# RWKV recurrence with 64x128 products of the write vectors, two VectorE steps that align the diagonal blocks, and another order of two GpSimd steps

## What is computed

```python
def step(state, inp):
    r_t, w_t, k_t, v_t, a_t, b_t = inp
    sa = jnp.einsum('bhvk,bhk->bhv', state, a_t)
    state = (state * w_t[:, :, None, :] + sa[..., None] * b_t[:, :, None, :]
             + v_t[..., None] * k_t[:, :, None, :])
    return state, jnp.einsum('bhvk,bhk->bhv', state, r_t)
```

## Time and profile before

| | |
|---|---|
| median of 3 runs | 1754.0 us (1753.24 to 1755.06) |
| the profiled execution | 1754.57 us, of which the traced span is 1752.8 us |
| PE busy | 1654.6 us, 94% of the span |
| DVE, ACT, POOL busy | 764.3, 561.3 and 452.3 us |
| mean granted clock of PE | 0.986 of full speed |
| first and last M0 of the recurrence | 153.0 and 432.5 us from the span's start |

### The profile page before, as it was taken

The page is one execution under the profiler, slowest core; times in us unless marked ns, Lnnn a source line. Parts: engine busy times, 40 slices in busy tenths (PEclk is TensorE's granted clock), DMA queues, the critical chain, the costliest instruction groups (busy, mean ns, idle before and its releaser), DMA issues. The chain is left out here.

```text
span 1752.8 us, 35509 instructions
## 1 busy us (share of the span) xinstructions
PE 1654.6 (94%) x15497; PEld 863.8 (49%) x15690; DVE 764.3 (44%) x1045; ACT 561.3 (32%) x883; POOL 452.3 (26%) x236
## 2 busy tenths in 40 slices
PE   4998889899999998899999999999999999999997
PEld 2455666666644555444444345444444444444443
DVE  5696555556425555312210388331323323222328
ACT  5323444444324555321212256321212112121200
POOL 2221322222110112022422123551423233232310
PEclk9999999999999999999999999999999999999999
DMA  9851001000101200411210211330202020212002
GB/s 358 285 175 32 15 6 38 4 27 27 28 25 49 61 1 1 137 44 36 72 36 24 96 49 37 103 129 21 85 20 76 24 72 26 70 36 84 1 0 97
DMA packets 105777, 109.75 MB, mean 63 GB/s; under 512 B 2592, under 2 KB 82610, under 8 KB 105394
## 3 DMA queue, kind: packets, MB, share of 16 engines
q1 hardware_dynamic: 105648, 107.82, 19.0%
HBM read 101.52 MB, written 4.19 MB: 60 GB/s over the span
## 5 line engine op out<-in xcount | busy, mean ns | idle before, releaser
L218 PE MATMUL tokens_ps<-a_hi,z 128*128 128x512 bf16 x878 | 228.5, 379 | 0.9
L674 PE MATMUL ff_ps<-ff_hi,c_lo 128*128 128x512 bf16 x503 | 190.6, 379 | 0.6
L674 PE MATMUL ff_ps<-ff_hi,c_hi 128*128 128x512 bf16 x501 | 189.9, 379 | 1.3 <-DVE z L2582 0.9
L674 PE MATMUL ff_ps<-ff_lo,c_hi 128*128 128x512 bf16 x501 | 189.9, 379 | 0.6
L2582 DVE TENSOR_TENSOR z<-ff_ps,z 128x512 f32<-128x512 f32 x128 | 88.3, 690 | 205.1 <-PE ff_ps L674 204.4
L2478 ACT ACTIVATE ff_r<-tokens_ps,cols 128x1024 f32<-128x1024 f32 x30 | 33.4, 1113 | 421.4 <-PE tokens_ps L218 414.4
L2404 POOL TENSOR_TENSOR z<-z 128x1024 bf16<-128x1024 f32 x28 | 62.1, 2219 | 345.5 <-ACT z L2400 345.5
L218 PEld LDWEIGHTS tokens_ps<-a_hi,z 128*128 128x128 bf16 x896 | 87.7, 98 | 105.7
L2570 DVE TENSOR_TENSOR ff_r<-ff_r 128x1024 f32<-128x1024 f32 x32 | 41.1, 1284 | 219.4 <-ACT ff_r L2478 219.4
L218 PE MATMUL tokens_ps<-a_lo,z 128*128 128x512 bf16 x438 | 131.1, 379 | 0.5
L195 POOL TENSOR_TENSOR mg_wlo<-mg_stage,mg_whi 128x1024 bf16<-128x1024 f32 x21 | 45.7, 2178 | 158.2 <-ACT mg_whi L191 158.2
(11 more groups left out here) (395 smaller groups left out, 3114.2 us busy)
## 6 DMA issues: line engine op xcount, KB each, us to landing
ff_st<-w_ff SPq DMA_DIRECT2D x8, 2048.0 KB, 7.7
z<-w_ff SPq DMA_DIRECT2D x30, 512.0 KB, 4.0
ada_w<-w_ada SPq DMA_DIRECT2D x6, 2048.0 KB, 8.3
z<-w_in SPq DMA_DIRECT2D x18, 512.0 KB, 4.9
z<-w_ada SPq DMA_DIRECT2D x8, 1024.0 KB, 13.4
mg_stage<-w_in SPq DMA_DIRECT2D x16, 512.0 KB, 3.9
zs_stage<-w_in SPq DMA_DIRECT2D x8, 512.0 KB, 7.3
ada_w<-w_ada SPq DMA_DIRECT2D x4, 1024.0 KB, 13.5
```

The lines of the kernel that those rows point to most:

```text
L218: last = pe.matmul(out[:, h * HALF:(h + 1) * HALF], w[:, kt, :], a[:, slot, h * HALF:(h + 1) * HALF], start=(x == 0 and y == 0), stop=(x = ...
L674: last = pe.matmul(out, a[:, slot, at], w[:, x, n], start=(x == 0 and y == 0), stop=(x == k - 1 and y == 2))
```

## The change

The 16 matmuls of L1808 and the 32 of L1817 become 16 matmuls of 64x128: each write vector of a chunk meets both read vectors, a and r, over all 64 tokens. The result therefore lies in the layout that M2 has, and VectorE reads it with another stride. The lower half of the rows has its diagonal block in columns 32 to 63 only. VectorE copies it over with two new operations ahead of L1507: `X` becomes the right half times a 0/1 column that keeps the lower rows, and the left half of `NTd` becomes itself times the opposite column, plus `X`. On GpSimd `dense_low(t + 2)` stands ahead of `low(t - 3)`.

```diff
--- before.py
+++ after.py
@@ -982,9 +982,9 @@
         zt, ysb, yc = sb("zt"), [sb(f"ysb{f}") for f in range(2)], [sb(f"yc{f}") for f in range(2)]
         BA, BB, BC, BD, F, TL, HY0, HY1 = (bank(n) for n in "main0 main1 inv invx front tail state0 state1".split())
         BAB, BCD, HY = (BA, BB), (BC, BD), (HY0, HY1)
-        per_turn = {"M1e": 2, "NTd": 2, "NTm": 2, "PQa": NT, "M2e": 2, "TTm": 2, "T12e": 2, "ze": 2, "ge": 2, "ysb": 2, "PQ": 2, "TTe": 4, "Te": 5, "X": 4, "Xe": 4, "TX": 4,
+        per_turn = {"nd": 2, "M1e": 2, "NTd": 2, "NTm": 2, "PQa": NT, "M2e": 2, "TTm": 2, "T12e": 2, "ze": 2, "ge": 2, "ysb": 2, "PQ": 2, "TTe": 4, "Te": 5, "X": 4, "Xe": 4, "TX": 4,
                     "ch": NC, "S": NC}
-        names = ("gs du draw dz dhi dlo vs vz vdif vcopy kkr sq lw sg la a cum cumE eN eE eI t k2 aN ss ssm rn AT RT BT KT wc rk BhT KhT M0 pp TT0 M1e NTd NTm TTe Te "
+        names = ("nd gs du draw dz dhi dlo vs vz vdif vcopy kkr sq lw sg la a cum cumE eN eE eI t k2 aN ss ssm rn AT RT BT KT wc rk BhT KhT M0 pp TT0 M1e NTd NTm TTe Te "
                  "M2 M2e X Xe TX X21 X21e TTm T12 T12e vnT vne knT kne bnT bne anT ane mv mve PQ PQa PQd ZG ze ge HY S0 ch S out ysb cen yc sqy "
                  "var sd ri rb y1 y2 bo bv gm y3 y4 yhi ylo vw vhi vlo vmm vout").split()
         s = {n: nc.alloc_semaphore(f"rws_{n}") for n in names}
@@ -1100,9 +1100,9 @@
             for t in range(TURNS):
                 if inside(t + 1):
                     front(t + 1)
+                dense_low(t + 2)
                 if inside(t - 3):
                     low(t - 3)
-                dense_low(t + 2)
                 if t >= TURNS - 2:
                     for kt in range((t - TURNS + 2) * PAIRS, (t - TURNS + 3) * PAIRS):
                         pool.wait_ge(s["vhi"], kt + 1)
@@ -1502,8 +1502,12 @@
                 wait(dve, t, "rn")
                 wait(dve, l, "TTm")
                 for e in range(2):
-                    dve.tensor_tensor(NTd[:, 4 * e:4 * e + 4, :], half4(BAB[e], 0), of_head(t, e, CH), ALU.mult).then_inc(s["NTd"], 1)
+                    dve.tensor_tensor(NTd[:, 4 * e:4 * e + 4, :], q4(BAB[e])[:, :, 0:CH], of_head(t, e, CH), ALU.mult).then_inc(s["NTd"], 1)
                 wait(dve, t, "NTd")
+                dve.tensor_scalar(X[:], NTd[:, :, B:CH], g.misc(6), None, ALU.mult).then_inc(s["nd"], 1)
+                wait(dve, t, "nd", 1)
+                dve.scalar_tensor_tensor(NTd[:, :, 0:B], NTd[:, :, 0:B], g.misc(5), X[:], ALU.mult, ALU.add).then_inc(s["nd"], 1)
+                wait(dve, t, "nd")
                 dve.tensor_tensor(TTs[:], NTd[:, :, 0:B], over(small(0), NB), ALU.mult).then_inc(s["pp"], 1)
                 wait(dve, t, "pp")
                 dve.tensor_tensor(TTs[:], TTs[:], over(eye, NB), ALU.add).then_inc(s["TT0"], 1)
@@ -1514,7 +1518,7 @@
                 dve.tensor_tensor(NTm[:], NTd[:, :, 0:B].unsqueeze(2).to_broadcast([P, NB, 3, B]), upper_levels, ALU.mult).then_inc(s["NTm"], 1)
                 queries(l, 0)
                 for e in range(2):
-                    dve.tensor_tensor(W[f][:, 4 * e:4 * e + 4, 0, :], half4(BAB[e], 1), over(incl, NT), ALU.mult).then_inc(s["M1e"], 1)
+                    dve.tensor_tensor(W[f][:, 4 * e:4 * e + 4, 0, :], q4(BAB[e])[:, :, CH:P], over(incl, NT), ALU.mult).then_inc(s["M1e"], 1)
                 inverse_deviation(lll)
                 state0(l)
                 write_hats(t)
@@ -1805,17 +1809,8 @@
                     for c2 in range(2):
                         at = (2 * j + c2) * CH
                         for e in range(2):
-                            pe.matmul(BAB[e][rows2[c2], (4 + j) * CH:(5 + j) * CH], bt[heads[e], at:at + CH], ar[f][heads[e], 1, at:at + CH],
-                                      start=True, stop=True)
-                for j in range(NT):
-                    for q in range(4):
-                        at, h = (2 * j + q // 2) * CH, q % 2
-                        for e in range(2):
-                            reads = ar[f][heads[e], 0, at:at + CH].rearrange("p (x n) -> p x n", x=2)
-                            if h:
-                                reads = ar[f][heads[e], 0, at + B:at + CH].unsqueeze(1).to_broadcast([HD, 2, B])
-                            last = pe.matmul(BAB[e][quads[q], j * CH:(j + 1) * CH].rearrange("p (x n) -> p x n", x=2),
-                                             bt[heads[e], at + h * B:at + h * B + B], reads, start=True, stop=True)
+                            last = pe.matmul(BAB[e][rows2[c2], j * P:(j + 1) * P].rearrange("p (x n) -> p x n", x=2), bt[heads[e], at:at + CH],
+                                             ar[f][heads[e], :, at:at + CH], start=True, stop=True)
                 last.then_inc(s["M0"], 1)
                 queries_maps(l)
                 state_terms(l)
```

## The result

The changed kernel takes 1743.87 us in the median of 4 runs (1742.76 to 1745.57) against 1754.34 for the kernel before; the ratio is 0.9942 with a 95% interval of [0.9924, 0.9959], so 10.2 us less of 1754 (the medians differ by 10.5). A second comparison of the same two files gave 0.9925 [0.991, 0.994], which is 13.2 us less. The forecast was 1740.5 us, with 1735 to 1748 as its range.

The account below looks back on a forecast made before the run. PE, busy 94% of the span, was taken as the bound, its M0 to M2 stretch going by instruction count. 7.3 + 1.8 + 4.5 + 0 = 13.6 us off 1754.0 gave 1740.4, stated as 1740.5; range 1735 to 1748.

Parts of the forecast that it names:

- Instructions: PE from M0 to M2: 128 of 795 instructions leave, gaining 7.3 us in turns 1 to 4, 1.8 in 5 and 6.
- I read the stops as PE having run through the instructions that are there: PE from M0 to M2: time goes by the number of instructions, not their columns; 2.17 us of 11.29 are stops.
- figure of 9.47 us: Expected time of each M0 to M2 stretch after the change: 667 instructions at 14.2 ns.
- 8.63 for the bare work: PE's work left per M0 to M2 stretch with all stops gone: 9.12 - 0.49 us.
- 14.2 ns per instruction: Rate on PE from M0 to M2: 11.29 us over 795 matmuls and weight loads.
- M0 itself: PE at M0: 1.41 us becomes 0.92 at full clock, 0.49 us less work a turn.
- tile count in the prediction: The Trainium skill's tiling rule at M0: both forms are 512 columns, so the merge would gain nothing.
- The first rival: PE's stops from M0 to M2 don't shrink: only 7.5 us gained, 1746.5 us; chance 0.18.
- GpSimd (4.5 us): Weights from L1097 come some 10 us earlier, so PE's three waits of 1.5 us go whole: 4.5 us gained.
- VectorE (0, with a cover of 0.4 us): Behind M0: the two new operations take 0.9 us, hidden behind PE's work, and cost nothing in turns 0 to 6.
- Turn 7: The VectorE pair costs up to 0.9 us there; with M0's gain of 0.34 us each in turns 0 and 7, about 0.
- What follows the recurrence: Later stages are PE's too and start earlier by as much as the recurrence gains; clock falls elsewhere may shift.

Follow-up runs that it names:

- count put back: Changed kernel with 32 one-column matmuls added ahead of each M0, so M0 has 48 matmuls again; ratio to the kernel before 0.9976 [0.9964, 0.9988].
- doubled: Changed kernel with 64 one-column matmuls ahead of each M0, 923 instructions from M0 to M2; ratio to the kernel before 1.0081 [1.0056, 1.0106].
- products only: Changed kernel with GpSimd's old order restored, keeping the new matmuls and VectorE's two operations; ratio to the kernel before 0.9957 [0.994, 0.9974].
- order-only kernel: Kernel before with only GpSimd's order changed; ratio to the kernel before 0.9978 [0.9967, 0.9989].
- old form at ends: Changed kernel with the old 48 matmuls and without VectorE's two operations in turns 0 and 7; ratio to the kernel before 0.9928 [0.9911, 0.9945].
- zt first: Changed kernel with VectorE's `queries(l, 1)` moved ahead of its two new operations; ratio to the kernel before 0.9928 [0.9913, 0.9942].
- ri first: Changed kernel with ScalarE's deviation (table load and square root for the logits) moved ahead of the gt copies; ratio to the kernel before 0.9928 [0.9914, 0.9942].
- second pair: Changed kernel with VectorE's two new operations done twice, values unchanged; ratio to the kernel before 0.9968 [0.9954, 0.9982].

## Why the prediction came out as it did

- **Instructions (forecast 7.3 and 1.8 us).** Measured 45.15 - 38.01 = 7.1 and 20.77 - 19.14 = 1.6 us. The mechanism, number and not columns, is shown by the count put back and doubled. The step "I read the stops as PE having run through the instructions that are there" is borne out too: 93 of 94 stops end 1.07 to 1.68 us after an instruction packet. But the figure of 9.47 us was luck in good part. In turns 1 and 2 stops come and go between 8.66 (the forecast had 8.63 for the bare work) and 10.14, so there is no steady 14.2 ns per instruction. In turns 3 to 6 the stops alone would leave some 9.0 to 9.5, and a chain through VectorE and ScalarE, which the forecast did not have, holds 9.5.
- **M0 itself (0.92 us).** It takes 0.89 to 0.93 us at full clock in turns 1 to 6. By the tile count in the prediction it should have gained nothing. The extra matmuls of one column fit what happened: each matmul record has a price of its own, 10 ns with its load, and M0 has lost 64 of them and 0.49 us. The clock was full in turns 5 and 6. This need not be the change's doing: with products only the idle 1.3 us at the start of these turns is back, and the mean clock is 1.00 there too.
- **The first rival, and the Trainium skill's rule (Runtime: NRT & Kernel Launch, section Instruction fetch mechanics) that the arrival of instructions is hidden.** Here they lose: 128 instructions without columns put 0.7 us of stops on the stretch beyond their own 0.64 us.
- **GpSimd (4.5 us).** In the order-only kernel 4.1 us, as worked out: L1097 ends 9 us ahead, `PQa` delays nobody. In the changed kernel the rests of turns 3, 4 and 5 lose 1.44, 0.53 and 1.44 us, 3.4 in all. The missing 0.9 us in turn 4 stands in both profiles, and with products only this turn is 0.9 us longer than its neighbours too (31.85). Of it 0.5 us is a stop within M2, from 0.65 to 1.15 us after its start: a stop given back just behind the window in which I counted them. It is no fixed cost of the products: in old form at ends, whose turns 1 to 6 have the same products, it is absent and the rest of turn 4 takes 29.49 us.
- **VectorE (0, with a cover of 0.4 us).** The pair's price was right, 0.90 for 0.9. The step that failed is "So 4.5 us are sure, `ge` will come at 4.1, and the cover is 0.4 us. It costs nothing in turns 0 to 6". With zt first, where nothing waits for `gt`, PE begins the correction 5.17 us after M0's start, 4.0 us after VectorE's first reading of M0, not 4.5. `gt` is there after 4.1. Why PE has 0.5 us less to do in between than the forecast read from turn 4 is not settled. In turn 0 PE waits 1.5 us for X, and what M0 gains there is lost (6.12 us from M0 to the correction against 6.06). And I had followed only the correction: ScalarE's table load and square root for the logits also stand behind `gt`. That it did not spoil the sum has a plain reason: with the waits taken away (zt first, ri first) no time of the kernel changed beyond the noise.
- **Turn 7 (about 0).** 10.34 and 8.79 us in two profiles, 9.39 before. "GpSimd does nothing in these stretches" was true of turns 1 to 6 and false of turn 7, where it works on the value weights (L1111, 417.94 to 422.45) while the pair's first operation runs and takes 1.02 us. That is not what made 10.34 us: in the second profile the same operation took 1.01 and the stretch 8.79.
- **What follows the recurrence (nothing lost).** The recurrence ends 12.0 us earlier (its last `queries_maps` starts at 453.62 instead of 465.58). Then 0.96 us is lost in the first 29 us of the next stage. Its windows after and before, from its first matmul to the same point:

```profile
517.08:546.88 29.80, 29.22 (x162) 14.50 (x162) 15.96 (x16) 12.71 (x30) 0.00 (x0) 0.89 0.26 71
```

```profile
529.02:557.86 28.84, 27.75 (x160) 14.04 (x163) 15.96 (x16) 12.71 (x30) 0.00 (x0) 0.94 0.26 73
```

  The same work at a mean clock of 0.89 instead of 0.94. PE was idle 3.0 us ahead of it in both. In the second profile of the changed kernel nothing is lost there: the recurrence ends 13.25 us earlier than before, and the span is 13.7 us shorter. Its recurrence also began 2.3 us later than that of the kernel before (M0 of turn 0 at 155.29, not 153.02), so from there to its end it took 15.5 us less, in the first profile 11.8. The forecast of 13.6 lies between them.

So the sum of 13.6 us met 10.2 the first time and 13.2 the second. Shown are the 7 to 8 us for the products, the 4 us for GpSimd's order, and the 0.9 us by which a second pair delays the correction in each turn. Which of the single stops falls in which turn stays open.

## What to carry to other kernels

Where PE runs hundreds of tiny matmuls in a row, count instructions ahead of columns: merging 48 matmuls into 16 took 1.8 us off the stretch in each of turns 1 to 4 and 7.5 us off eight turns, and adding matmuls of one column gave it back. A rate such as 14 ns an instruction includes stops that come and go; take it as a mean and keep a range of 1.5 us a stretch around it. When stops of the bound engine go, what was hidden behind them is bare at once; work out the cover from that engine's work alone, and follow all that is queued behind the delayed result on the other engines too. If one of two independent steps on an idle engine is waited for and the other waits, put the first ahead.

## What the runs showed of the hardware

- A matmul of 64x32 weights that streams a single column still costs PE 10 ns a matmul record with its load (64 of them in 0.64 us, count put back).
- PE's stops named "issue" end with instruction packets: 93 of 94 stops over 0.3 us, in thirteen traces, ended 1.07 to 1.68 us after a 16 KiB packet of queue q8 had ended.
- Stops in a dense run of small instructions vary between executions of one program: 8.66 or 10.14 us for the same 667 instructions.
- VectorE's TENSOR_SCALAR on 128x256 f32 takes 0.35 us, and 1.02 and 1.01 us (two profiles) in turn 7, where GpSimd is at work.
- An idle time of PE of 1.3 to 1.5 us was followed by 1.2 GHz in turns 5 and 6 of the kernel before and not in its turn 4, nor in any of the three with products only.
